# Wide products for the hi weights in the second feed-forward layer and the gated MLP, and a halved last block

## The chip, the cores and the metric

The kernel runs on one core of a Trainium2 chip. The metric is the device time in microseconds (us). TensorE (PE in the profile; PEld is its weight load) multiplies, VectorE (DVE) and ScalarE (ACT) work element by element, GpSimd (POOL) takes small powers and issues a few loads, SyncE (SP) issues the loads of the weights.

## What is computed

For 256 tokens of width 1024: a first block (feed-forward layer, a mixer of Fourier and differential attention branches, feed-forward layer, norm) and a second one (a gated MLP with token mixing, chunked attention, norm). The change touches two parts:

```python
def swiglu(x, wg, wu, wd):                       # 1024 -> 2816 -> 1024, used twice in the first block
    return (jax.nn.silu(x @ wg) * (x @ wu)) @ wd

def gmlp_mixer(h, w_in, ln_g, ln_b, w_s, b_s, w_out):
    u, v, z = jnp.split(h @ w_in, 3, axis=-1)    # 2048 each
    u = gelu(u); v = layer_norm(gelu(v), ln_g, ln_b)
    mixed = einsum('hts,bgshc->bgthc', masked w_s, v) + b_s
    return (u * mixed * silu(z)) @ w_out
```

## The kernel before

Every float32 operand is used as a sum of two parts of the faster type fp32r: hi (a copy in that type) and lo (what is left). A product of w and x is then three products: hi of w with hi of x, hi of w with lo of x, lo of w with hi of x. Weights pass in blocks of 1024 x 256 (or 256 x 1024), 1 MB each: SyncE loads a block into one of four `raw` buffers, ScalarE copies it into `hi` (`hi`, L290), VectorE subtracts it into `lo` (`lo`, L295); four slots of hi and lo each. A block's place in the order of all blocks is `NTH[...]`; the semaphores `hi`, `lo` and `used` count blocks. `hi` of block n waits until block n-4 has been multiplied.

The second feed-forward layer (`pe_ffn` with "ffn2") has 11 iterations. Iteration i multiplies gate block i into bank G and up block i into bank U (`to_features`, L330 to L332: for each half f of the block's 256 channels and each of 8 slices k of the width, three products of 256 columns, the tokens), then contracts down block i-1 with h of iteration i-1 into the four banks pAcc (`contract`, L380, 24 products of 512 columns). ScalarE takes silu of G into `stage_a`; VectorE multiplies U with it into h (L1526); ScalarE and VectorE split h into `h_hi` and `h_lo` (L930, L1329). Iteration 0 has the tokens as rows (`pair_to_tokens`), with gate and up block side by side in one product of 512 columns; its h is transposed through bank M in iteration 1. After the last iteration `contract_last` takes the first token tile of the last but one block (12 products), then the last block, whose h must be split by then; the turn to the next stage (residual sum, norm, transposes) is woven into it.

The gated MLP (`pe_gmlp`) first makes v (`vgate`, products of 512 columns in which xT is loaded and the weights of two blocks, two runs of 256, stream), then has 8 iterations: z block into G, transposition of W_s of this iteration into bank R (`w_s_transposed`, L691, plain float32), u block into U, mixing of tokens into bank M (`mix`, L701, plain float32, four products), contraction of block i-1. ScalarE: silu(z), a table load for gelu, gelu(u), a table load back. VectorE (`gated`): gelu(u) times silu(z) (L1770), b_s added to M (L1774), product of the two to h (L1778); then LayerNorm slices of the next v (`v_ln`), `lo` steps and the copies of W_s transposed (`w_s`). GpSimd loads the next W_s (L1925) once the last one is transposed, and the next LayerNorm slices (L1921) once b_s has been added; these stand in one queue in that order.

ScalarE, VectorE and GpSimd each follow an order written out by hand, and an instruction that waits holds all behind it.

Of the kernel before, what the change touches and what calls it, by code (L numbers as in the profile page):

```python
# [8 lines left out]
P = 128  # L9
TOK = 256  # L10
# [57 lines left out]
PAIR0 = {"mixin": 1, "ffn2": 2, "vgate": 3, "chunk": 7}  # L68
UNITS = [(0, 0), (0, 1), (1, 0), (1, 1), (2, 0), (2, 1), (4, 0), (4, 1), (3, 0), (3, 1),
# [15 lines left out]
def squares_done(g, t):  # L85
# [20 lines left out]
    "silu": "first gate (bank G) -> SA", "act_b": "second gate (bank U) -> SB", "h": "h in SBUF",  # L106
    "warm": "tables loaded ahead", "hh": "hi part of h", "hl": "lo part of h", "hT": "h of token-major blocks transposed",
# [20 lines left out]
    "a_mix": "tokens mixed", "a_zu": "b_s added", "a_ss": "gelu(u) * silu(z)",  # L128
# [8 lines left out]
def build(nc, T, out):  # L137
# [3 lines left out]
    with ctx:  # L141
# [21 lines left out]
        XT = [sb("xT_hi", KD * TOK, f32r), sb("xT_lo", KD * TOK, f32r)]  # L163
# [40 lines left out]
        BST = at("v_stats", NT * 4 * 6, f32, a0 + 14 * KB)  # L204

# [114 lines left out]
        def to_features(pe, n, bank, x, k0=0, nk=KD, half_way=0):  # L320

            wh, wl = v3(HI[n % NHL][:, :], KD), v3(LO[n % NHL][:, :], KD)
            for f in range(2):
                o = bank[:, f * TOK:(f + 1) * TOK]
# [133 lines left out]
        def pe_ffn(pe, ph, q, after=None):  # L458

            for i in range(NF):  # L460
# [14 lines left out]
                else:  # L475
                    if (ph, i) == ("ffn2", 1):
                        pe.wait_ge(S["pair_h"], 1)
                    else:
                        pe.wait_ge(S["silu"], H0[ph] + i)
                    to_features(pe, n, G, XT).then_inc(S["used"], 1)  # L480
                    pe.wait_ge(S["lo"], n + 2)
                    pe.wait_ge(S["h"], H0[ph] + i)
# [6 lines left out]
                    to_features(pe, n + 1, U, XT).then_inc(S["used"], 1)  # L489
# [172 lines left out]
        def pe_gmlp(pe):  # L662
# [31 lines left out]
            def mix(i):  # L694
# [4 lines left out]
                for h in range(2):  # L699
                    for g in range(NT):  # L700
                        end = pe.matmul(M[:, h * TOK + g * P:h * TOK + (g + 1) * P],  # L701
                                        VL[i % 2][:, g * BC + h * P:g * BC + (h + 1) * P], WT[:, h * P:(h + 1) * P],
                                        start=True, stop=True)
                end.then_inc(S["a_mix"], 1)

            for i in range(8):
# [4 lines left out]
                if i == 1:  # L711

                    mix(0)
# [4 lines left out]
                if i:  # L718
                    mix(i)
                if 0 < i < 7:  # L720
                    contract(pe, "gmlp", i - 1)
            contract_last(pe, "gmlp", 4)
# [242 lines left out]

        def act_ffn(act, ph):
            for i in range(NF):
# [31 lines left out]
            h_hi(act, ph, NF - 1)  # L999
# [187 lines left out]
        def act_gmlp(act):  # L1187
# [11 lines left out]
            for i in range(8):  # L1199
                n = NTH["gmlp", "z", i]  # L1200
                if i > 1:
                    hi(act, n + 3)
# [4 lines left out]
                if i != 1:  # L1207
# [3 lines left out]
                if i < 7:  # L1211
                    warm(act, ACT.Silu)
                    hi(act, n + 5)
                if i == 0:
                    hi(act, n + 6)
                h_hi(act, "gmlp", i)

# [283 lines left out]

        def dve_ffn(dve, ph):
            for i in range(NF):
# [229 lines left out]
        def dve_gmlp(dve):  # L1733
# [32 lines left out]

            def gated(i):
                dve.wait_ge(S["silu"], H0["gmlp"] + i + 1)
                dve.wait_ge(S["act_b"], ACT_B0["gmlp"] + i + 1)
                dve.tensor_tensor(SB[:, :], SB[:, :], SA[:, :], ALU.mult).then_inc(S["a_ss"], 1)  # L1770
                dve.wait_ge(S["a_mix"], i + 1)
                m4, x4 = (v[:, :].rearrange("p (h g t) -> p h g t", h=2, g=NT) for v in (M, MX))
                b_s = v3(APAR[i % 2][:, 2 * BC:3 * BC], 2).unsqueeze(2).broadcast_to([P, 2, NT, P])
                dve.tensor_tensor(x4, m4, b_s, ALU.add).then_inc(S["a_zu"], 1)  # L1774
                dve.wait_ge(S["a_ss"], i + 1)
                dve.wait_ge(S["a_zu"], i + 1)
                dve.wait_ge(S["hl"], H0["gmlp"] + i)
                dve.tensor_tensor(H[:, :], MX[:, :], SB[:, :], ALU.mult).then_inc(S["h"], 1)  # L1778

# [24 lines left out]
            lo(dve, n + 5)  # L1804
            gated(0)
# [3 lines left out]
            for i in range(1, 8):  # L1809
                n = NTH["gmlp", "z", i]  # L1810
                gated(i)
                if i < 7:
                    v_ln(i + 1)
                    lo(dve, n + 5)
                    h_lo(dve, "gmlp", i)
                    lo(dve, n + 6)
                    w_s(i + 1)
                    lo(dve, n + 7)
                else:
                    h_lo(dve, "gmlp", i)  # L1820
# [197 lines left out]
        def _(act):  # L2018
# [24 lines left out]
            act_ffn(act, "ffn2")  # L2043
            act_pair(act, NTH["vgate", "v", 0])
# [6 lines left out]
        def _(dve):  # L2051
# [16 lines left out]
            dve_ffn(dve, "ffn2")  # L2068
            dve_pair(dve, NTH["vgate", "v", 0])
# [39 lines left out]
```

## Time and profile before

| | us |
|---|---|
| Median of three runs | 883.17 (882.92 to 883.72) |
| Profiled execution | 882.84 |
| Its span, first to last instruction | 881.0 |
| TensorE busy in it | 867.2 (98%) |
| VectorE, ScalarE, GpSimd busy | 588.2, 479.5, 61.3 |

The profile is one execution. A line of a timeline gives start, length, engine, line of the kernel, operation, output and inputs; a product of TensorE runs into the next one, so what a product costs is the distance from one start to the next, not its length. "Idle before" is time in which the engine had nothing to do, with the instruction that ended it.

### The profile page before, as it was taken

The page shows a single profiled execution, that of the slowest core. Times are in us where ns is not written, and L with a number is a line of the kernel's source. Part 1 is how long each engine was busy: PE and PEld are TensorE (multiplying, and loading weights), DVE is VectorE, ACT ScalarE, POOL GpSimd, SP SyncE. Part 2 cuts the span into 40 slices and gives each one's busy share as a digit, 9 for nine tenths or more (in the row PEclk, how much of TensorE's full clock was granted, in tenths as well). Part 3 has the DMA queues.
Part 4 walks back from the last instruction along what each step waited for, and adds up shares of the span by engine and source line. Part 5 has one row for each costly group of instructions (what it writes and reads, how often), then busy time and mean ns, then how long its engine had stood idle before and what let it go on. Part 6 is the DMA issues. An engine that isn't in the chain of part 4 may idle for free. (4 is left out here: it accounts for less than half of the span.)

```text
span 881.0 us, 14413 instructions
## 1 busy us (share of the span) xinstructions
PE 867.2 (98%) x6150; PEld 809.1 (92%) x6150; DVE 588.2 (67%) x635; ACT 479.5 (54%) x591; POOL 61.3 (7%) x69
## 2 busy tenths in 40 slices
PE   7999999999999999999999999999999999999997
PEld 7999999998999999899999997989999997999995
DVE  5797988987587655655445457658766567666663
ACT  6667576656574443543443446447654645675652
POOL 0022223210000000000000000100000001000001
PEclk9999999999999999999999999999999999999999
DMA  9865556565644655556555655776656655854301
GB/s 299 303 201 188 191 191 192 181 204 156 201 145 138 197 192 167 174 185 195 187 191 181 202 165 170 224 248 221 218 188 213 219 149 174 264 167 156 121 1 48
DMA packets 124224, 163.14 MB, mean 185 GB/s; under 512 B 3969, under 2 KB 110977, under 8 KB 124161
## 3 DMA queue, kind: packets, MB, share of 16 engines
q1 hardware_dynamic: 122320, 155.41, 54.3%
q0 software_dynamic: 1552, 6.29, 2.1%
q8 instruction: 48, 0.79, 0.4%
q10 hardware_dynamic: 288, 0.52, 0.2%
q14 instruction: 16, 0.12, 0.0%
HBM read 161.17 MB, written 1.05 MB: 184 GB/s over the span
## 5 line engine op out<-in xcount | busy, mean ns | idle before, releaser
L295 DVE TENSOR_TENSOR lo<-raw,hi 128x2048 fp32r<-128x2048 f32 x131 | 299.1, 2288 | 136.2 <-ACT hi L290 136.1
L290 ACT ACTIVATE hi<-raw 128x2048 fp32r<-128x2048 f32 x140 | 265.3, 1905 | 28.7 <-DMA raw<-in_ffn_wd 7.2
L330 PE MATMUL pU<-xT_hi,hi 128*128 128x256 f32 x608 | 173.2, 285 | 0.0
L331 PE MATMUL pU<-xT_lo,hi 128*128 128x256 f32 x608 | 172.0, 283 | 0.0
L332 PE MATMUL pU<-xT_hi,lo 128*128 128x256 f32 x608 | 172.0, 283 | 0.0
L330 PE MATMUL pG<-xT_hi,hi 128*128 128x256 f32 x544 | 154.1, 283 | 0.0
L332 PE MATMUL pG<-xT_hi,lo 128*128 128x256 f32 x544 | 153.9, 283 | 0.0
L331 PE MATMUL pG<-xT_lo,hi 128*128 128x256 f32 x544 | 153.9, 283 | 0.0
L330 PEld LDWEIGHTS pU<-xT_hi,hi 128*128 128x128 f32 x608 | 116.6, 192 | 0.2
L331 PEld LDWEIGHTS pU<-xT_lo,hi 128*128 128x128 f32 x608 | 116.6, 192 | 0.0
L332 PEld LDWEIGHTS pU<-xT_hi,lo 128*128 128x128 f32 x608 | 116.6, 192 | 0.0
L330 PEld LDWEIGHTS pG<-xT_hi,hi 128*128 128x128 f32 x544 | 104.3, 192 | 1.5 <-issue 0.3
L331 PEld LDWEIGHTS pG<-xT_lo,hi 128*128 128x128 f32 x544 | 104.3, 192 | 1.1
L332 PEld LDWEIGHTS pG<-xT_hi,lo 128*128 128x128 f32 x544 | 104.3, 192 | 0.0
L930 ACT ACTIVATE h_hi<-h 128x512 fp32r<-128x512 f32 x28 | 17.7, 632 | 124.5 <-PE pAcc L380 119.1
L380 PE MATMUL pAcc<-hi,h_hi 128*128 128x512 f32 x240 | 74.9, 393 | 0.0
L380 PE MATMUL pAcc<-lo,h_hi 128*128 128x512 f32 x240 | 74.2, 390 | 0.0
L380 PE MATMUL pAcc<-hi,h_lo 128*128 128x512 f32 x240 | 74.0, 389 | 0.0
L380 PEld LDWEIGHTS pAcc<-hi,h_lo 128*128 128x128 f32 x240 | 45.1, 188 | 9.7
L380 PEld LDWEIGHTS pAcc<-lo,h_hi 128*128 128x128 f32 x240 | 45.0, 188 | 9.7
L888 POOL TENSOR_TENSOR stats<-stats,minus_half 128x1 f32<-128x1 f32 (+2 forms) x15 | 9.7, 647 | 580.7 <-DVE stats L882 275.6
L380 PEld LDWEIGHTS pAcc<-hi,h_hi 128*128 128x128 f32 x240 | 43.1, 189 | 7.1
(377 smaller groups left out, 1472.1 us busy)
## 6 DMA issues: line engine op xcount, KB each, us to landing
raw<-in_a_w_in SPq DMA_DIRECT2D x24, 1024.0 KB, 5.2
raw<-in_ffn_wd SPq DMA_DIRECT2D x22, 1024.0 KB, 5.0
raw<-in_ffn_wg SPq DMA_DIRECT2D x21, 1024.0 KB, 5.3
raw<-in_ffn_wu SPq DMA_DIRECT2D x21, 1024.0 KB, 5.3
raw<-in_w_in SPq DMA_DIRECT2D x16, 1024.0 KB, 5.4
raw<-in_a_w_out SPq DMA_DIRECT2D x8, 1024.0 KB, 5.0
raw<-in_w_kv SPq DMA_DIRECT2D x8, 1024.0 KB, 5.6
raw<-in_b_w_qz SPq DMA_DIRECT2D x8, 1024.0 KB, 5.7
```

Source lines behind the costliest of these rows:

```text
L290: act.activation(HI[n % NHL][:, :], RAW[n % NRAW][:, :], ACT.Copy).then_inc(S["hi"], 1)
L295: dve.tensor_tensor(LO[n % NHL][:, :], RAW[n % NRAW][:, :], HI[n % NHL][:, :].bitcast(f32), ALU.subtract).then_inc(S["lo"], 1)
L330: pe.matmul(o, wk, xh, start=(k == 0), stop=False)
L331: pe.matmul(o, wk, xl, start=False, stop=False)
L332: end = pe.matmul(o, wl[:, k0 + k, f * P:(f + 1) * P], xh, start=False, stop=(k == nk - 1))
L380: end = pe.matmul(ACC[2 * t + c][:, :], a, w[:, r, c * 512:(c + 1) * 512], start=(i == 0 and r == 0 and m == 0), stop=False, skip_group_ch ...
L888: pool.tensor_tensor(ST[:, c:c + w], ST[:, c:c + w], HALF[:, 0:w], ALU.pow).then_inc(S["rsqrt"], 1)
L930: act.activation(h_parts(ph, i)[0][:, :], H[:, :], ACT.Copy).then_inc(S["hh"], 1)
```

## The change

1. Wide products. In ffn2 from iteration 1 (gate) and 2 (up) on, and in the gated MLP from iteration 2 on (z, and u except the last), a block is multiplied by `wide_to_features`: hi of w meets hi and lo of x in one product of 512 columns (two runs of 256, 8 KB apart) into the whole of a bank, and lo of w meets hi of x in one of 256 columns onto the bank's left half. So each half f of a block has its own bank: gate (G, U), up (M, R), z (G, R), u (U, M). ScalarE copies the right half of each bank to SBUF (`wide_act`), VectorE adds the left half to it (`wide_dve`); silu, gelu and the products read the sum in `WG` or `WU`. 30 blocks are wide. Up block 1 goes to R by the old way.
2. Gated MLP, order. `mix(i)` writes bank G and stands with `w_s_transposed(i+1)` between u and the contraction; W_s of the next iteration is transposed there and no longer between z and u. VectorE adds b_s and multiplies with silu(z) first (`mixed`), and with gelu(u) afterwards (`gated`). The orders of `hi` and `lo` steps on ScalarE and VectorE change with it.
3. Last block of the gated MLP: `mix(7)` stands between z and u; u's halves go to banks U and R; gelu, h and its split are done a half at a time (`gated_last`).

```diff
-        XT = [sb("xT_hi", KD * TOK, f32r), sb("xT_lo", KD * TOK, f32r)]
+        XT_ALL = sb("xT", 2 * KD * TOK, f32r)
+        XT = [XT_ALL[:, c * KD * TOK:(c + 1) * KD * TOK] for c in range(2)]
...
+        def wide_to_features(pe, b, banks, free):
+            n = NTH[b]
+            wh, wl = v3(HI[n % NHL][:, :], KD), v3(LO[n % NHL][:, :], KD)
+            x4 = XT_ALL[:, :].rearrange("p (c k t) -> p c k t", c=2, k=KD)
+            for f, bank in enumerate(banks):
+                pe.wait_ge(*free[f])
+                for k in range(KD):
+                    w = slice(f * P, (f + 1) * P)
+                    pe.matmul(v3(bank[:, :], 2), wh[:, k, w], x4[:, :, k, :], start=(k == 0), stop=False,
+                              skip_group_check=True)
+                    end = pe.matmul(bank[:, 0:TOK], wl[:, k, w], x4[:, 0, k, :], start=False, stop=(k == KD - 1),
+                                    skip_group_check=True)
+                end.then_inc(S["used" if f else "wide"], 1)
...
+            mix(1, M)
+            w_s_transposed(2)
+            contract(pe, "gmlp", 0)
+            for i in range(2, 8):
+                z, u = ("gmlp", "z", i), ("gmlp", "u", i)
+                pe.wait_ge(S["lo"], NTH[z] + 1)
+                wide_to_features(pe, z, (G, R), ((S["silu"], H0["gmlp"] + 2) if i == 2 else (S["a_zu"], i),
+                                                 (S["a_wt"], 2 * (i + 1))))
+                pe.wait_ge(S["lo"], NTH[u] + 1)
+                if i < 7:
+                    wide_to_features(pe, u, (U, M), ((S["act_b"], ACT_B0["gmlp"] + 2), (S["a_zu"], 2)) if i == 2 else
+                                     [summed(("gmlp", "u", i - 1), f) for f in range(2)])
+                    pe.wait_ge(*summed(z, 0))
+                    mix(i, G)
+                    pe.wait_ge(*summed(z, 1))
+                    w_s_transposed(i + 1)
                     contract(pe, "gmlp", i - 1)
+                else:
+                    pe.wait_ge(*summed(("gmlp", "u", 6), 1))
+                    mix(7, M)
+                    pe.wait_ge(*summed(("gmlp", "u", 6), 0))
+                    pe.wait_ge(*summed(z, 1))
+                    to_features(pe, NTH[u], U, XT, other=R, first_half="wide").then_inc(S["used"], 1)
...
+        def wide_act(act, b, banks, dst, f):
+            if f:
+                act.wait_ge(S["used"], NTH[b] + 1)
+            else:
+                act.wait_ge(S["wide"], NTHW[b] + 1)
+            act.activation(dst[:, f * TOK:(f + 1) * TOK], banks[f][:, TOK:512], ACT.Copy).then_inc(S["wide_r"], 1)
+        def act_ffn2(act):
+            for i in range(1, NF):
+                gate, up = ("ffn2", "gate", i), ("ffn2", "up", i)
+                n = NTH[gate]
+                hi(act, n + LEAD)
+                act.wait_ge(S["h"], H0["ffn2"] + i)
+                wide_act(act, gate, (G, U), WG, 0)
+                wide_act(act, gate, (G, U), WG, 1)
+                if i == 1:
+                    h_hi(act, "ffn2", 0)
+                hi(act, n + 1 + LEAD)
+                act.wait_ge(*summed(gate, 1))
+                act.activation(SA[:, :], WG[:, :], ACT.Silu).then_inc(S["silu"], 1)
+                if i > 1:
+                    wide_act(act, up, (M, R), WU, 0)
+                    wide_act(act, up, (M, R), WU, 1)
+                if i < NF - 1:
+                    h_hi(act, "ffn2", i)
+                    hi(act, n + 2 + LEAD)
+            h_hi(act, "ffn2", NF - 1)
...
+        def wide_dve(dve, b, banks, dst, f):
+            dve.wait_ge(S["wide_r"], 2 * NTHW[b] + f + 1)
+            o = dst[:, f * TOK:(f + 1) * TOK]
+            dve.tensor_tensor(o, banks[f][:, 0:TOK], o, ALU.add).then_inc(S["wide_sum"], 1)
...
+            def gated_last():
+                dve.wait_ge(S["a_ms"], 8)
+                dve.wait_ge(S["last_u"], 1)
+                dve.wait_ge(S["hl"], H0["gmlp"] + 7)
+                dve.tensor_tensor(H[:, 0:TOK], MX[:, 0:TOK], SB[:, 0:TOK], ALU.mult).then_inc(S["last_h"], 1)
+                dve.wait_ge(S["last_hh"], 1)
+                dve.tensor_tensor(HL_LAST[:, 0:TOK], H[:, 0:TOK], HH_LAST[:, 0:TOK].bitcast(f32),
+                                  ALU.subtract).then_inc(S["last_hl"], 1)
...
+            for i in range(2, 8):
+                z, u = ("gmlp", "z", i), ("gmlp", "u", i)
+                n = NTH[z]
+                lo(dve, n + 3)
+                wide_dve(dve, z, (G, R), WG, 0)
+                wide_dve(dve, z, (G, R), WG, 1)
+                lo(dve, n + 4)
+                if i == 7:
+                    mixed(7, M)
+                    gated_last()
+                    break
+                wide_dve(dve, u, (U, M), WU, 0)
+                wide_dve(dve, u, (U, M), WU, 1)
+                mixed(i, G)
+                gated(i)
+                w_s(i + 1)
+                v_ln(i + 1)
+                lo(dve, n + 5)
+                h_lo(dve, "gmlp", i)
```

## Rows read from the trace of the kernel before

**Rows 1.** The page, busy time of the engines.
```profile
PE 867.2 (98%) x6150; PEld 809.1 (92%) x6150; DVE 588.2 (67%) x635; ACT 479.5 (54%) x591; POOL 61.3 (7%) x69
```
**Rows 2.** Waits of PE: who for whom, us in total, times, longest.
```profile
PE pAcc L380 <- DVE h_lo_last L1329: 1.1, 2, 0.8
PE pG L429 <- DVE xn L1698: 1.0, 1, 1.0
```
**Rows 3.** Timeline of PE, ffn2: up block starts, contraction starts, next gate starts.
```profile
509.65 0.28 PE L330 MATMUL pU<-xT_hi,hi 128*128 128x256 f32 x1
...
515.41 0.63 PE L380 MATMUL pAcc<-hi,h_hi 128*128 128x512 f32 x2
...
520.88 0.28 PE L330 MATMUL pG<-xT_hi,hi 128*128 128x256 f32 x1
```
**Rows 4.** Timeline of PE: 96 vgate products to z0; chunk's 24; chunk's K block.
```profile
569.58 0.40 PE L358 MATMUL pAcc<-hi,xT_hi 128*128 128x512 f32 x1
...
591.37 0.28 PE L330 MATMUL pG<-xT_hi,hi 128*128 128x256 f32 x1
...
744.56 0.40 PE L358 MATMUL pAcc<-hi,xTk_hi 128*128 128x512 f32 x1
...
750.16 1.04 PE L429 MATMUL pAcc<-ident,xn 128*128 128x128 f32 x8
...
752.02 0.28 PE L331 MATMUL pG<-xTk_lo,hi 128*128 128x256 f32 x1
...
757.58 0.28 PE L330 MATMUL pU<-xT_hi,hi 128*128 128x256 f32 x1
```
**Rows 5.** Timeline of PE, gated MLP's last iteration: u, mix, contractions of blocks 6 and 7.
```profile
718.44 0.36 PE L330 MATMUL pU<-xT_hi,hi 128*128 128x256 f32 x1
718.88 0.28 PE L330 MATMUL pU<-xT_hi,hi 128*128 128x256 f32 x1
...
724.27 1.05 PE L701 MATMUL pM<-wsT,v_ln 128*128 128x128 f32 x8
725.08 0.70 PE L380 MATMUL pAcc<-hi,h_hi 128*128 128x512 f32 x2
...
728.90 0.47 PE L380 MATMUL pAcc<-hi,h_hi_last 128*128 128x512 f32 x1 [0.82 <-DVE h_lo_last L1329]
```
**Rows 6.** Timelines of ACT and DVE in the same stretch.
```profile
724.47 0.60 ACT L1210 ACTIVATE stage_b<-pU 128x512 f32<-128x512 f32 x1 [2.05 <-PE pU L332]
...
728.06 0.69 DVE L1329 TENSOR_TENSOR h_lo_last<-h,h_hi_last 128x512 fp32r<-128x512 f32 x1 [0.70 <-ACT h_hi_last L930]
```
**Rows 7.** Timelines of ACT and DVE, ffn2's iteration 0: instructions on 256 columns of a bank.
```profile
367.82 0.39 ACT L978 ACTIVATE stage_a<-pU 128x256 f32<-128x256 f32 x1 [3.72 <-PE pU L360]
...
368.24 0.42 DVE L1522 TENSOR_TENSOR h<-pU,stage_a 128x256 f32<-128x256 f32 x1 [2.08 <-ACT stage_a L978]
```
**Rows 8.** Timelines of DVE, ACT and PE at the end of ffn2.
```profile
532.65 0.69 DVE L1526 TENSOR_TENSOR h<-pU,stage_a 128x512 f32<-128x512 f32 x1 [1.03 <-PE pU L332]
534.04 0.69 DVE L1329 TENSOR_TENSOR h_lo_last<-h,h_hi_last 128x512 fp32r<-128x512 f32 x1 [0.70 <-ACT h_hi_last L930]
...
533.37 0.63 ACT L930 ACTIVATE h_hi_last<-h 128x512 fp32r<-128x512 f32 x1 [4.08 <-DVE h L1526]
...
535.14 0.39 PE L380 MATMUL pAcc<-hi,h_hi_last 128*128 128x512 f32 x1
```
**Rows 9.** Load of W_s 2 in GpSimd's timeline, landing of all such loads, mix(1).
```profile
611.72 0.70 POOL L1925 DMA_DIRECT2D ws<-in_a_w_s  x1
...
DMA to landing us min/median/max: 4.4/5.4/8.0
...
615.71 1.05 PE L701 MATMUL pM<-wsT,v_ln 128*128 128x128 f32 x8
```
**Rows 10.** The page, costliest groups: busy us, mean ns | idle before, releaser.
```profile
L295 DVE TENSOR_TENSOR lo<-raw,hi 128x2048 fp32r<-128x2048 f32 x131 | 299.1, 2288 | 136.2 <-ACT hi L290 136.1
L290 ACT ACTIVATE hi<-raw 128x2048 fp32r<-128x2048 f32 x140 | 265.3, 1905 | 28.7 <-DMA raw<-in_ffn_wd 7.2
```

More of the change, by code:

```diff
@@ L68 @@
 PAIR0 = {"mixin": 1, "ffn2": 2, "vgate": 3, "chunk": 7}
+WIDE = [("ffn2", "gate", 1)] + [("ffn2", k, i) for i in range(2, NF) for k in ("gate", "up")]
+WIDE += [("gmlp", k, i) for i in range(2, 7) for k in ("z", "u")] + [("gmlp", "z", 7)]
+NTHW = {b: n for n, b in enumerate(WIDE)}
 UNITS = [(0, 0), (0, 1), (1, 0), (1, 1), (2, 0), (2, 1), (4, 0), (4, 1), (3, 0), (3, 1),
@@ L106 @@
     "silu": "first gate (bank G) -> SA", "act_b": "second gate (bank U) -> SB", "h": "h in SBUF",
+    "wide": "wide blocks half multiplied", "wide_r": "right halves of their banks -> SBUF",
+    "wide_sum": "left halves added to them (2 a block)",
+    "last_u": "second gate, first half of the last block of a phase", "last_h": "its h", "last_hh": "hi part", "last_hl": "lo part",
+    "a_ms": "mixed tokens times silu(z)",
     "warm": "tables loaded ahead", "hh": "hi part of h", "hl": "lo part of h", "hT": "h of token-major blocks transposed",
@@ L127 @@
     "a_wt": "and in SBUF (2 parts)", "a_vg": "(v - mean) * gain (2 tiles)", "a_vs": "v after LayerNorm (2 tiles)",
-    "a_mix": "tokens mixed", "a_zu": "b_s added", "a_ss": "gelu(u) * silu(z)",
+    "a_mix": "tokens mixed", "a_zu": "b_s added",
     "b_hb": "relative bias loaded", "b_mask": "chunk mask in it", "b_k": "K -> SBUF", "b_q": "Q -> SBUF",
@@ L488, in pe_ffn @@
                         end.then_inc(S["hT"], 1)
-                    to_features(pe, n + 1, U, XT).then_inc(S["used"], 1)
+                    if ph == "ffn1" or i == 1:
+                        to_features(pe, n + 1, U if ph == "ffn1" else R, XT).then_inc(S["used"], 1)
+                    else:
+                        free = [(S["h"], H0[ph] + 2)] * 2 if i == 2 else [summed((ph, "up", i - 1), f) for f in range(2)]
+                        wide_to_features(pe, (ph, "up", i), (M, R), free)
                 if 0 < i < NF - 1:
@@ L692, in w_s_transposed, with mix @@
                 end.then_inc(S["a_wt_ps"], 1)
-            def mix(i):
+            def mix(i, bank):
                 pe.wait_ge(S["a_vs"], 2 * (i + 1))
@@ L704, in mix @@
                 end.then_inc(S["a_mix"], 1)
-            for i in range(8):
+            for i in range(2):
                 n = NTH["gmlp", "z", i]
@@ L711, in pe_gmlp @@
                 if i == 1:
-                    mix(0)
+                    mix(0, M)
                 w_s_transposed(i)
@@ L1198, in act_gmlp @@
                 hi(act, n + 5)
-            for i in range(8):
+            for i in range(2):
                 n = NTH["gmlp", "z", i]
-                if i > 1:
-                    hi(act, n + 3)
                 act.wait_ge(S["used"], n + 1)
@@ L1808, in dve_gmlp @@
             lo(dve, n + 6)
-            for i in range(1, 8):
-                n = NTH["gmlp", "z", i]
-                gated(i)
[L1812 to L1820, printed above, removed]
+            n = NTH["gmlp", "z", 1]
+            mixed(1, M)
+            gated(1)
+            w_s(2)
+            v_ln(2)
+            lo(dve, n + 5)
+            h_lo(dve, "gmlp", 1)
+            for i in range(2, 8):
+                z, u = ("gmlp", "z", i), ("gmlp", "u", i)
+                n = NTH[z]
+                lo(dve, n + 3)
[9 more added lines that the diff above has]
+                mixed(i, G)
+                gated(i)
+                w_s(i + 1)
+                v_ln(i + 1)
+                lo(dve, n + 5)
+                h_lo(dve, "gmlp", i)
         def b_softmax(dve, i):
```

116 lines of the change are left out of this document (90 added, 26 removed).

## The prediction

> **What bounds the kernel now.** I read the page first: TensorE is busy for 867.2 of 881.0 us, the others for two thirds of it at most [rows 1]. A busy TensorE need not be at its peak, so next the waits: it waits for others for about a microsecond at a time, at the turns between stages [rows 2], and never inside the iterations. The kernel is a chain of TensorE's products, and the time changes by what the products cost from start to start and by waits that come or go at a few places. The start-to-start cost is read from timelines. In ffn2 an up block of 48 narrow products (256 columns) runs from 509.65 to 515.41: 5.76 us, 120 ns each; a contraction of 24 products of 512 columns runs from there to 520.88: 5.47 us, 228 ns each [rows 3]. A product of twice the columns is thus 12 to 13 ns cheaper than two narrow ones: each carries a fixed part of about 13 ns, whatever its length.
>
> **Wide products.** A step (one k, one f) is 3 x 120 = 360 ns now. The narrow product that stays costs 120 ns. The wide one streams two runs of 256 columns of xT. Nothing now streams xT in 512 columns; the nearest rows are vgate's, with the operands in the opposite roles but with two runs: 96 products from 569.58 to 591.37, 227 ns each [rows 4]. So 227 + 120 = 347 ns, 13 ns less. Steps: ffn2 19 blocks, gated MLP 11, 16 steps a block, 480 in all: 480 x 13 ns = 6.24 us less. Bounds: at the start of the chunk stage the same form costs 233 ns (24 products, 744.56 to 750.16), and the narrow products that follow 118 (47 of them, 752.02 to 757.58) [rows 4], so 6 to 15 ns a step, 2.9 to 7.2 us; at the worst, two narrow ones' 240, nothing. I take vgate's value, since xT and the slots of hi and lo lie where they lie now; chunk's row has another buffer (xTk). The change from a wide to a narrow product is taken at no extra cost: the contraction's 228 and the block's 120 include such borders [rows 3].
>
> **The new copies and sums.** A wide block adds two ScalarE copies of 256 columns, 0.39 us each, and two VectorE sums, 0.42 us [rows 7]: 1.6 us an iteration on each engine in ffn2. They are off TensorE's path if they are done before the bank is needed. In ffn2 (time from the iteration's start): h_hi, which waits for the contraction, then a hi step of 1.9 us (down block), another 1.9 (the next gate block), so ScalarE is free at about 4.4; gate's second half ends at 5.6, is copied by 6.1, and VectorE, which by then has its lo steps of 2.3 us [rows 10] done at 7.0, has summed at 7.8. TensorE needs G and U again at 16.6. The hi and lo steps queued behind these waits (up i+1, down i) end at 8.0 and 10.3, and at 2.4 and 4.7 of the next iteration; they are needed when TensorE reaches those blocks, at 22 and 28. 6 us or more of cover everywhere, so nothing. SyncE's loads wait for lo steps, which come no later than now. In the gated MLP the nearest need is z's sums, behind which mix(i) now stands in TensorE's queue: ready at 6.6, wanted at 11.1. If this 4.5 us were gone, each us more would be TensorE's.
>
> **One switch less.** The first fp32r product after a float32 one holds the engine longer: u's first three take 0.44 us (718.44 to 718.88) where three take 0.36 elsewhere [rows 5], so 0.08. W_s is now transposed next to mix, six times: 6 x 0.08 = 0.48 us less (between 0 and 0.6).
>
> **The last block of the gated MLP.** Now from u's end (724.27) to the contraction of block 7 (728.90) pass 4.63 us: mix 0.81, a switch 0.08, 12 products of 0.228 = 2.73, and 1.01 of wait and restart [rows 5]. With mix ahead of u and halves, after u come gelu (starts 0.20 after u's end [rows 6]), h, hi, lo, each on 256 columns, about 0.4 with 0.04 between them, and 0.15 until TensorE starts (728.06 + 0.69 to 728.90 [rows 5, 6]): 2.1 us, under 2.73. So the 1.01 goes. But TensorE must wait before u for the sum of z's second half: 0.20 + 0.39 + 0.04 + 0.42 + 0.15 = 1.20 after z's end, of which mix covers 0.81: 0.39 us more. Net 0.62 less.
>
> **The turn of ffn2.** Its last h isn't halved, and a copy (0.39), a sum (0.42) and handoffs (0.07 to 0.09) now stand before it: 0.88 us. h_lo ends at 534.73, TensorE takes up the last block at 535.14 [rows 8]; after the 0.15 there are 0.26 us of cover. The rest, 0.62, is a wait of TensorE. But the chain of the turn on ScalarE and VectorE (hi, lo, residual sums, norm) starts from h_hi and is late by 0.88, and TensorE waits for its end already now (1.0 us for xn [rows 2]). So all 0.88 us count.
>
> **W_s of block 2.** It was transposed inside iteration 2; now TensorE wants it right behind mix(1), at 615.71 + 0.81 = 616.52. GpSimd issues its load at 611.72, after the LayerNorm slices that wait for b_s being added; 5.4 us to landing: 617.1 [rows 9]. VectorE adds b_s a little earlier (the product that stood before it moves behind), at most 0.7. Behind the wait stands the contraction of block 0. Landing between 4.4 and 8.0 us [rows 9] gives 0 to 3.2 us; I take 0.7. Later W_s have an iteration of cover.
>
> **Sum.** -6.24 - 0.48 - 0.62 + 0.88 + 0.7 = -5.76 us. The profiled execution took 882.84 us around a span of 881.0, and the median is 883.17, 0.33 more. So a profile of 877.1 and a median of 877.4.
>
> **Rivals.** (A) The sum as it stands: 877.4. Chance 0.73.
> (B) The wide product costs what chunk's does, 233 to 234 ns: a step saves 6 ns, 480 x 6 = 2.9 us instead of 6.24: 880.8. For it: the same form has both prices in one trace, so the price hangs on where the operands lie, and xT has never streamed this way. Against: xT's narrow products cost as much streamed as loaded, 120. Chance 0.13.
> (C) The fixed 13 ns isn't saved: it belongs to 256 columns that stream (a run, or the weight load beside it), and the wide product costs 240. Then only the other terms are left: -0.48 - 0.62 + 0.88 + 0.7 = +0.5, so 883.7, no change. Against: vgate's and the contraction's rows both have 227 to 228. Chance 0.09.
> The Trainium skill, in "TensorE: Matmul & The Clock Gate", section "Back-to-back issue gap", gives a warm product its columns at 2.4 GHz plus a fixed 2.5 ns. By that a step saves 2.5 ns, an estimate of 1.2 us for 480 steps, and the time would be 882.5. The trace disagrees at 256 and 512 columns alike (120 and 227 ns against the page's 109 and 216); only the size of the part that goes with a product differs.
> (D) Slower: late sums. In the gated MLP z's sums stand behind a hi and a lo step, and mix, W_s and the contraction behind the sums. If weight blocks land late, each us beyond the 4.5 of cover falls on TensorE. ScalarE waited 7.2 us for a load once in this trace [rows 10]; at that lateness in each of the five iterations 2 to 6 it is 2.7 x 5 = 13.5 us: 890.9. It decides from 6.0 us of lateness an iteration (1.5 x 5 = 7.5 beyond the cover makes it slower by 0.2%). Against: the 28.7 us that ScalarE waits at hi steps are spread over 140. Chance 0.05.
>
> **Range and chances.** About 0.2% (1.8 us) is what a measurement of this kernel can tell from no change. Within (A), the narrow product at 118 and no wait for W_s take off 1.7, a W_s load at its slowest adds 2.5. The range reaches to (B): 875.2 to 881.0. Faster: (A), (B): 0.86. Same: (C): 0.09. Slower: (D): 0.05.
>
> **What the profile would show.** A block of z or gate takes 5.55 us instead of 5.76 from its first start to the next block's; in (B) 5.66, in (C) 5.76. No wait of TensorE inside the iterations; an iteration of ffn2 16.6 us instead of 17.0. Waits of TensorE: about 0.6 for h_lo_last in ffn2 and none in the gated MLP; 1.2 for xn; one for the sum of z 7 (0.4); one behind mix(1) (0.7), before a W_s transposition. The prediction is wrong if the wide products have a price of their own, or if TensorE waits at each mix.

## The result, and the profile after

| | before | after |
|---|---|---|
| median (lowest to highest), 7 runs each | 883.48 us (882.91 to 883.72) | 880.00 us (879.87 to 880.64) |
| profiled execution: time, span | 882.84, 881.0 us | 880.00, 878.2 us |

The ratio is 0.9963, with a 95% interval of 0.9954 to 0.9973: 0.4% faster, by 3.5 us between the medians (2.4 to 4.1 by the interval). The forecast was 877.4, the range 875.2 to 881.0. The time lies in the range, but near rival (B)'s 880.8 and not at the point.

The page of after, the engines' busy time (before: [rows 1]), and its waits of PE (before: [rows 2]):

```profile
PE 865.6 (99%) x5670; PEld 784.5 (89%) x5670; DVE 610.5 (70%) x697; ACT 500.1 (57%) x653; POOL 61.2 (7%) x69
```

```profile
PE pG L463 <- DVE xn L1844: 1.2, 1, 1.2
PE pAcc L414 <- DVE h_lo_last L1443: 0.7, 2, 0.4
```

480 products fewer, and TensorE busy for 1.6 us less: the products that went gave back little. The timeline of PE in ffn2 (columns as in [rows 3]); gate block's first bank, four products in the middle of it, up block's first bank, contraction, next gate block:

```profile
401.85 0.39 PE L359 MATMUL pG<-xT,hi 128*128 128x512 f32 x1
...
402.54 0.40 PE L359 MATMUL pG<-xT,hi 128*128 128x512 f32 x1
402.78 0.28 PE L361 MATMUL pG<-xT,lo 128*128 128x256 f32 x1
402.90 0.40 PE L359 MATMUL pG<-xT,hi 128*128 128x512 f32 x1
403.14 0.28 PE L361 MATMUL pG<-xT,lo 128*128 128x256 f32 x1
...
407.49 0.40 PE L359 MATMUL pM<-xT,hi 128*128 128x512 f32 x1
...
413.14 0.64 PE L414 MATMUL pAcc<-hi,h_hi 128*128 128x512 f32 x2
...
418.65 0.39 PE L359 MATMUL pG<-xT,hi 128*128 128x512 f32 x1
```

A wide block takes 5.64 us (401.85 to 407.49) and 5.65 (to 413.14), where 5.55 was forecast, 5.66 for rival (B), and 5.76 was the narrow one's [rows 3]; an iteration takes 16.80 us (401.85 to 418.65), where 16.6 was forecast. A step is 11.29 / 32 = 353 ns: in the rows a wide product is followed after 240 ns and a narrow one after 120. The exact starts in the trace repeat over three steps, 236 + 113, 233 + 117, 241 + 120 ns. So a wide product between narrow ones costs 233 to 241 ns, and the narrow one 117 on average, where vgate's row had promised 227 and the block's row 120.

Where the 2.8 us of the two spans went is read from landmarks. Of before, rows that don't stand above: start of gate 1, of the last contraction pair of ffn2, of the norm's transpositions, of z 2, and the end of z 7 (the W_s transposition behind it):

```profile
367.62 0.28 PE L330 MATMUL pG<-xT_hi,hi 128*128 128x256 f32 x1
...
532.39 0.63 PE L380 MATMUL pAcc<-hi,h_hi 128*128 128x512 f32 x2
...
543.11 0.66 PE L429 MATMUL pG<-ident,xn 128*128 128x128 f32 x4 [1.00 <-DVE xn L1698]
...
622.09 0.28 PE L330 MATMUL pG<-xT_hi,hi 128*128 128x256 f32 x1
...
718.31 0.38 PE L691 MATMUL pR<-ident,ws 128*128 128x128 f32 x2
```

The same landmarks of after, with the start of the last block's contraction in ffn2 and, at the end of the gated MLP, mix(7), u 7, and the contractions of blocks 6 and 7:

```profile
367.77 0.39 PE L359 MATMUL pG<-xT,hi 128*128 128x512 f32 x1
...
530.70 0.40 PE L414 MATMUL pAcc<-hi,h_hi 128*128 128x512 f32 x1
...
534.00 0.47 PE L414 MATMUL pAcc<-hi,h_hi_last 128*128 128x512 f32 x1 [0.36 <-DVE h_lo_last L1443]
...
542.23 0.44 PE L463 MATMUL pG<-ident,xn 128*128 128x128 f32 x2 [1.18 <-DVE xn L1844]
...
621.42 0.39 PE L359 MATMUL pG<-xT,hi 128*128 128x512 f32 x1
...
716.50 1.05 PE L742 MATMUL pM<-wsT,v_ln 128*128 128x128 f32 x8
717.68 0.36 PE L342 MATMUL pU<-xT,hi 128*128 128x256 f32 x1
...
723.50 0.63 PE L414 MATMUL pAcc<-hi,h_hi 128*128 128x512 f32 x2
...
726.25 0.39 PE L414 MATMUL pAcc<-hi,h_hi_last 128*128 128x512 f32 x1
```

| stretch | before | after | difference |
|---|---|---|---|
| start of the kernel to gate 1 | 367.62 | 367.77 | +0.15 |
| ffn2's iterations (19 wide blocks), to the last contractions | 164.77 | 162.93 | -1.84 |
| turn, to the norm's transpositions | 10.72 | 11.53 | +0.81 |
| to z 2 (holds W_s 2's transposition in after) | 78.98 | 79.19 | +0.21 |
| gated MLP, z 2 to z 7's end (11 wide blocks) | 96.22 | 95.08 | -1.14 |
| to the contraction of block 7 (holds W_s 7's in before) | 10.59 | 9.75 | -0.84 |
| to the end | 152.1 | 151.95 | -0.15 |

The sum is -2.80. The two stretches with wide blocks give 2.98, where 6.24 (and 0.48 for the merge) were forecast.

### The profile page after: what moved, and what is told of

Its sections match the earlier page's. It is cut to its first block, busy times and chain, and to the rows that moved or that the text cites. A ratio compares the mean times of both kernels' runs of the same rounds, so it can differ in the third digit from the quotient of the medians.

```text
span 878.2 us, 13599 instructions
## 1 busy us (share of the span) xinstructions
PE 865.6 (99%) x5670; PEld 784.5 (89%) x5670; DVE 610.5 (70%) x697; ACT 500.1 (57%) x653; POOL 61.2 (7%) x69
## 4 chain that ended last, share of the span: by engine, by line
PE 94%; DVE 3%; DMA 1%; ACT 1%; issue 1%; SPq 0%; POOL 0%; POOLq 0%; DVEq 0%
PE pAcc L414 22%; PE pU L342 5%; PE pU L343 5%; PE pU L344 5%; PE pG L342 5%; PE pG L344 5%; PE pG L343 5%; PE pG L359 3%; PE pU L359 3%; PE pR L359 3%; PE pM L359 3%; PE pG L361 2%; PE pAcc L392 2%; PE pAcc L393 2%; PE pAcc L394 2%; PE pU L361 2%
## 5 line engine op out<-in xcount | busy, mean ns | idle before, releaser
L342 PE MATMUL pU<-xT,hi 128*128 128x256 f32 x360 | 102.5, 285 | 0.1
L343 PE MATMUL pU<-xT,hi 128*128 128x256 f32 x360 | 101.8, 283 | 0.0
L344 PE MATMUL pU<-xT,lo 128*128 128x256 f32 x360 | 101.8, 283 | 0.0
L342 PE MATMUL pG<-xT,hi 128*128 128x256 f32 x288 | 81.7, 284 | 0.0
L344 PE MATMUL pG<-xT,lo 128*128 128x256 f32 x288 | 81.5, 283 | 0.0
L343 PE MATMUL pG<-xT,hi 128*128 128x256 f32 x288 | 81.5, 283 | 0.0
L342 PEld LDWEIGHTS pU<-xT,hi 128*128 128x128 f32 x360 | 69.0, 192 | 0.5 <-DVE wide_gate L1620 0.3
L343 PEld LDWEIGHTS pU<-xT,hi 128*128 128x128 f32 x360 | 69.1, 192 | 0.0
L344 PEld LDWEIGHTS pU<-xT,lo 128*128 128x128 f32 x360 | 69.0, 192 | 0.0
L342 PEld LDWEIGHTS pG<-xT,hi 128*128 128x128 f32 x288 | 55.2, 192 | 0.8 <-issue 0.3
L343 PEld LDWEIGHTS pG<-xT,hi 128*128 128x128 f32 x288 | 55.2, 192 | 0.5
L344 PEld LDWEIGHTS pG<-xT,lo 128*128 128x128 f32 x288 | 55.2, 192 | 0.0
L1443 DVE TENSOR_TENSOR h_lo<-h,h_hi 128x512 fp32r<-128x512 f32 x28 | 19.3, 688 | 48.9 <-ACT h_hi L990 48.9
```

Of the source, the lines that this page charges most:

```text
L1443: dve.tensor_tensor(b[:, :], src[:, :], a[:, :].bitcast(f32), ALU.subtract).then_inc(S["hl"], 1)
```

## The experiments

"The kernel before" was run beside each group: its median was 883.51 us beside e1 to e4, 883.62 beside e5 to e8, 883.15 beside e9 to e11 and 883.08 beside e12. Every ratio is to the kernel before of the same group. "Theory" with a number or letter means the one of that name in the expectation just above. The diffs are shortened.

**e1_grouped.** Is it the alternation of wide and narrow products?

```diff
                 for k in range(KD):
                     w = slice(f * P, (f + 1) * P)
                     pe.matmul(v3(bank[:, :], 2), wh[:, k, w], x4[:, :, k, :], ...)
+                for k in range(KD):
                     end = pe.matmul(bank[:, 0:TOK], wl[:, k, w], x4[:, 0, k, :], ...)
```

> The changed kernel, but in each half of a wide block the eight wide products come first and the eight narrow ones after them. In the changed kernel a step of one wide and one narrow product costs 353 ns (236 and 117), where 347 (227 and 120) were forecast. Theory 1: the price comes from the alternation of the two lengths. Then eight wide ones in a row cost 227 each and the narrow ones 120, a block 5.55 us instead of 5.65, and the time is 880.0 - 30 x 0.10 = 877. Theory 2: it comes from what the wide product streams (two runs of xT, 8 KB apart). Then a wide one costs 234 or more in a row as well, a block stays at 5.65 and the time at 880.0.

Measured: 877.47 us (877.45 to 877.99), ratio to before 0.9935 (0.9919 to 0.9952), 2.5 us under the changed kernel. The timeline of PE, same iteration:

```profile
401.51 1.98 PE L359 MATMUL pG<-xT,hi 128*128 128x512 f32 x8
403.33 1.11 PE L362 MATMUL pG<-xT,lo 128*128 128x256 f32 x8
404.28 2.00 PE L359 MATMUL pU<-xT,hi 128*128 128x512 f32 x8
406.12 1.12 PE L362 MATMUL pU<-xT,lo 128*128 128x256 f32 x8
...
412.66 0.63 PE L415 MATMUL pAcc<-hi,h_hi 128*128 128x512 f32 x2
```

Behind the 512-column contraction eight wide products take 1.82 us, 227 ns each, just as vgate's did; eight narrow ones 0.95; behind these, eight wide ones 1.84. Two blocks are 11.15 us. So the wide product of this xT has vgate's price in a run, and it is the alternation with shorter products that costs.

**e2_one_run.** Is it the two runs of 256 columns? The wide product streams 512 adjacent columns instead: hi, or lo, of two neighbouring slices k. The sizes stay, but the sums are no longer the product that the kernel should make.

```diff
-                    pe.matmul(v3(bank[:, :], 2), wh[:, k, w], x4[:, :, k, :], ...)
+                    pe.matmul(bank[:, :], wh[:, k, w], XT_ALL[:, k * 512:(k + 1) * 512], ...)
```

> The changed kernel, but the wide product streams 512 columns that lie in one run (hi or lo of two neighbouring slices k) instead of hi and lo of one slice: the same sizes on wrong data, so what the blocks compute is not the product. Theory 1 (alternation): a step stays at 353 ns. Theory 2 (two runs): 347 ns, a block 5.55 us, the time 877.

Measured: 879.97 us (a single run), a span of 878.2, the changed kernel's to the tenth, and the starts repeat as there (233 + 118, 241 + 120, 236 + 113 ns). The form of the operand has no price here.

**e3_split.** The change without its wide products: each is two narrow ones again, all else is as changed.

```diff
-                    pe.matmul(v3(bank[:, :], 2), wh[:, k, w], x4[:, :, k, :], ...)
+                    pe.matmul(bank[:, 0:TOK], wh[:, k, w], x4[:, 0, k, :], ...)
+                    pe.matmul(bank[:, TOK:512], wh[:, k, w], x4[:, 1, k, :], start=False, ...)
```

> The changed kernel with all its orders, banks, copies and sums, but each wide product is made as two narrow ones. If only the products carry the gain, a wide block is back at 5.76 us (3 x 120 a step) and the time is 880.0 + 30 x 0.105 = 883.2, the same as the kernel before: the rest (turn of ffn2 +0.8, last block of the gated MLP -0.7) cancels out. Rival: the orders and the halved block gained something that the products do not show; then the time is under 882.5.

Measured: 884.49 us (884.04 to 885.3), ratio 1.0014 (1.0004 to 1.0023), 0.98 us over before and 1.3 over the 883.2 expected, which had left out the wait for W_s 2 (0.9, below). The prediction's terms without the products and the merge give +0.88 - 0.62 + 0.7 = +0.96. That the medians meet this sum is in part chance, since the term for W_s is 0.9 here and not 0.7: GpSimd's timeline, then PE's.

```profile
612.66 0.71 POOL L2107 DMA_DIRECT2D ws<-in_a_w_s  x1
```

```profile
616.87 1.05 PE L744 MATMUL pM<-wsT,v_ln 128*128 128x128 f32 x8
618.64 0.44 PE L734 MATMUL pR<-ident,ws 128*128 128x128 f32 x2 [0.72 <-DMA ws<-in_a_w_s]
```

Mix to W_s is 1.77 us, 0.9 more than mix alone takes in after (0.88, below); from its issue to its use the load had 6.0 us. The stretch from the norm's transpositions to z 2 is 80.13 us, 0.94 more than in after. Of the 4.5 us between this kernel and the changed one, this is 0.9; the two stretches with wide blocks (164.77 and 96.29 us) are 3.05 longer, and that is what the wide products bring, 6.4 ns a step.

**e4_last_up_narrow.** The turn of ffn2: the last up block goes the old way, into bank R, with no copy and no sum ahead of h (this line picks the wide blocks; the products, ScalarE's copies and VectorE's h follow it).

```diff
-WIDE = [("ffn2", "gate", 1)] + [("ffn2", k, i) for i in range(2, NF) for k in ("gate", "up")]
+WIDE = [("ffn2", "gate", 1)] + [("ffn2", k, i) for i in range(2, NF) for k in ("gate", "up") if (k, i) != ("up", NF - 1)]
```

> The changed kernel, but the last up block of ffn2 is multiplied the old way, into one bank (R), and VectorE takes h from that bank without copy and sum. If the 0.8 us that the turn of ffn2 lost come from copy and sum in front of the last h, the last contraction starts 2.75 us after the up block as in the kernel before and the transpositions 0.81 us earlier; the block costs 0.1 more: 879.3. If the turn is held by something else, 880.1.

Measured: 879.65 us (879.54 to 880.06), ratio 0.9959 (0.9944 to 0.9974). Timeline of PE:

```profile
530.71 0.63 PE L414 MATMUL pAcc<-hi,h_hi 128*128 128x512 f32 x2
...
533.46 0.39 PE L414 MATMUL pAcc<-hi,h_hi_last 128*128 128x512 f32 x1
...
541.42 0.66 PE L463 MATMUL pG<-ident,xn 128*128 128x128 f32 x4 [1.00 <-DVE xn L1846]
```

The turn is 10.71 us again, as in before (10.72) and not as in after (11.53), and the wait for h_lo_last is gone. So the copy and the sum are what delayed the turn. The median shows 0.35 of these 0.8 us, too little to tell from after by the ratios alone; the landmarks account for it. The narrow block costs 0.1 more, and the stretch to z 2 is 0.4 longer (79.58 us against 79.19), since in this execution TensorE waited for W_s 2 (0.2 us in its list of waits).

**e5_whole_block, e6_block_and_last, e7_fours.** How the price of alternation is made up. e5 has all 16 wide products of a block first, then the 16 narrow ones; e6 is e5 with the narrow last up block of e4.

```diff
             for f, bank in enumerate(banks):
                 pe.wait_ge(*free[f])
                 for k in range(KD):
                     pe.matmul(v3(bank[:, :], 2), wh[:, k, f * P:(f + 1) * P], x4[:, :, k, :], ...)
+            for f, bank in enumerate(banks):
+                for k in range(KD):
                     end = pe.matmul(bank[:, 0:TOK], wl[:, k, f * P:(f + 1) * P], x4[:, 0, k, :], ...)
```

> In every wide block the 16 wide products (both halves, both banks) come first and the 16 narrow ones after them; nothing else differs from the changed kernel. Theory 1, the price lies at each return from narrow to wide products: in the trace of the kernel with halves grouped, the first five wide products after eight narrow ones took 233, 236, 228, 233 and 230 ns and the first narrow one 113, so one return costs 25 - 7 = 18 ns. A block has one return instead of two, 30 blocks x 18 ns = 0.5 us less than the grouped kernel's 877.5: 876.9. Theory 2, the price lies in how long the second bank's narrow half is kept open or in late sums (a first half is ready 1.9 us later): no gain or a loss, 877.5 or more, with waits of TensorE inside the iterations.

> The kernel of e5_whole_block, and the last up block of ffn2 multiplied in the old narrow way into bank R, so that nothing stands between its second gate and h. If the two gains are independent: the turn gives back what it gave in the kernel with the last up block narrow (879.65 against 880.0, 0.35), so 0.35 less than e5_whole_block, 876.5; TensorE waits 0.3 for h_lo_last once (gates stage) instead of twice. If the turn is set by another chain after grouping, it equals e5_whole_block.

e7 has the groups of e1 cut in two (k 0 to 3 wide, then narrow, then k 4 to 7):

```diff
-                for k in range(KD):
+                for k0 in (0, KD // 2):
+                    for k in range(k0, k0 + KD // 2):
```

> Groups of four: in each half 4 wide, 4 narrow, 4 wide, 4 narrow products; four returns to wide a block instead of two (grouped) or sixteen (changed kernel). Theory 1a, each return costs 18 ns as read from the grouped kernel's trace: 30 blocks x 2 x 18 ns = 1.1 us over 877.5: 878.6, a block of 5.60 us. Theory 1b, the price is the same for each return, 880.0 - 877.5 = 2.5 us over 30 x 14 returns = 6 ns: 877.9, a block of 5.57 us.

| | returns from narrow to wide for each block | median, us (lowest to highest) | ratio to before |
|---|---|---|---|
| e5 | 1 | 876.84 (876.76 to 877.55) | 0.9926 (0.9914 to 0.9939) |
| e6 | 1 | 876.82 (876.58 to 877.19) | 0.9925 (0.9912 to 0.9937) |
| e1 | 2 | 877.47 (877.45 to 877.99) | 0.9935 (0.9919 to 0.9952) |
| e7 | 4 | 878.59 (878.21 to 878.95) | 0.9944 (0.9931 to 0.9958) |
| changed kernel | 16 | 880.00 (879.87 to 880.64) | 0.9963 (0.9954 to 0.9973) |

(A gate or z block follows a contraction, also of 512 columns, and has one return less than the table says.) e5 and e7 came out as theory 1 and 1a had it (876.9 and 878.6): each return costs about 18 ns as long as the runs are four or more long (20 from e1 to e5 and 15 from e1 to e7, by the two stretches with wide blocks), and where every product is a return it is 6 ns a step, 96 a block. The rows of e5, an up block, and of e7, a half gate block:

```profile
406.82 2.00 PE L358 MATMUL pM<-xT,hi 128*128 128x512 f32 x8
408.66 1.98 PE L358 MATMUL pR<-xT,hi 128*128 128x512 f32 x8
410.47 1.12 PE L362 MATMUL pM<-xT,lo 128*128 128x256 f32 x8
```

```profile
401.45 1.07 PE L360 MATMUL pG<-xT,hi 128*128 128x512 f32 x4
402.36 0.64 PE L363 MATMUL pG<-xT,lo 128*128 128x256 f32 x4
402.83 1.09 PE L360 MATMUL pG<-xT,hi 128*128 128x512 f32 x4
403.76 0.63 PE L363 MATMUL pG<-xT,lo 128*128 128x256 f32 x4
```

In e5, 1.84 us for the eight behind narrow ones, 1.81 for the eight behind wide ones; in e7 0.91 for four behind the contraction, 0.93 for four behind narrow ones. e6 should have been at 876.5; at 0.02 under e5 its last narrow block shows no gain that can be told. Its turn is 0.82 us shorter than e5's (10.71 against 11.53), but ffn2's iterations are 0.19 longer with the narrow block (161.09 against 160.90), and the stretch to z 2, in which it waited for W_s 2 and e5 did not, 0.40 (79.64 against 79.24). What is left, 0.23, is less than the runs of one kernel scatter.

**e8_before_moved.** The prediction had seen the same product at 227 and at 233 and put it on the operands' place. Both kernels allocate xT on a multiple of 128 bytes (worked out from the order and sizes of the regions); xTk begins 96 bytes past one. Here the kernel before has xT moved by 32 bytes.

```diff
+        region(32)
         XT = [sb("xT_hi", KD * TOK, f32r), sb("xT_lo", KD * TOK, f32r)]
+        region(32)
```

> The kernel before, with 32 bytes left free ahead of xT_hi and 32 behind xT_lo, so that xT begins 32 bytes past a multiple of 64 as xTk does; every other buffer behind them stays on its place modulo 64. Theory P, the place of the streamed buffer sets the price (xTk: 118 and 233 ns; xT: 120 and 227 ns): a narrow block of 48 goes from 5.76 to 5.68 us, some 75 blocks, 6 us less, the 168 products of vgate and mixin that stream xT's partner or use it as weights change at most 1 us: 877 to 879. Theory Q, the place plays no part: 883.5, narrow products still 120 ns.

Measured: 875.77 us (875.62 to 876.14), ratio 0.9912 (0.9897 to 0.9927): 7.9 us from 64 bytes of padding, more than twice what the change brings. It is theory P, and 1.2 us under the least that P gave: the narrow product falls to 117 ns and not 118.

```profile
410.16 0.62 PE L382 MATMUL pAcc<-hi,h_hi 128*128 128x512 f32 x2
...
415.75 0.28 PE L332 MATMUL pG<-xT_hi,hi 128*128 128x256 f32 x1
```

The narrow block (404.56 to 410.16) takes 5.60 us, 117 ns a product; but the contraction takes 5.59 instead of 5.47 [rows 3]. h_hi and h_lo had moved by 64 bytes with everything behind xT.

**e9_before_xt_only, e10_after_xt_only, e11_best_xt_only.** xT alone is moved, in the kernel before, in the changed kernel, and in e6.

```diff
-        XT = [sb("xT_hi", KD * TOK, f32r), sb("xT_lo", KD * TOK, f32r)]
...
+        HALF = sb("minus_half", 4)
+        XT = [sb("xT_hi", KD * TOK, f32r), sb("xT_lo", KD * TOK, f32r)]
         IDENT = sb("ident", P)
         ST = sb("stats", 112)
-        HALF = sb("minus_half", 4)
```

> The kernel before, with xT alone on another place: it is allocated behind h_lo and the 32 bytes of minus_half, so it begins 32 bytes past a multiple of 128, and hi, lo, h_hi, h_lo and everything from xTk on keep their places modulo 2048. In e8_before_moved everything behind xT had also moved by 64 bytes, and the products of the contractions took 231 and 236 ns in turn instead of 227. Theory H, that price came with the moved h_hi and h_lo: narrow products of xT at 117, contractions at 227 again, 720 products x 5 ns = 3.6 us less than e8's 875.8: 872.2. Theory X, xT's place alone sets the state of all: contractions stay at 233, 875.8.

> The changed kernel with the same move of xT. Theory 1, the gain of the wide product hangs on xT's place: where a narrow product takes 117, two of them take 234, what a product of 512 columns takes there (231 to 236), so the wide products save nothing and what is left of the change is what e3_split showed (+1.2 us against before at most, W_s load and start in it): e9_before_xt_only plus 0 to 1.2 us. Theory 2, the fixed part of a product is saved wherever xT lies: 3 to 6 us under e9_before_xt_only.

> The fastest order so far (wide products of a block first, narrow ones after, last up block of ffn2 narrow) with the same move of xT. Theory 1: grouping saves nothing either, as no wide product is cheaper than two narrow ones there: within 0.5 us of e10_after_xt_only. Theory 2: 3 us under e10_after_xt_only, as 876.8 is under 880.0 on the old place.

| | median, us (lowest to highest) | ratio to before |
|---|---|---|
| e9, narrow | 872.40 (872.37 to 872.65) | 0.9877 (0.9863 to 0.9892) |
| e10, wide, alternating | 871.58 (871.11 to 871.93) | 0.9869 (0.9852 to 0.9885) |
| e11, wide, grouped | 873.20 (872.70 to 873.73) | 0.9886 (0.9871 to 0.9901) |

Timelines of PE in ffn2: e9 (up block, contraction, next gate), e10 (a half block, contraction), e11 (16 wide, then 8 narrow).

```profile
402.35 0.28 PE L330 MATMUL pU<-xT_hi,hi 128*128 128x256 f32 x1
...
407.94 0.63 PE L380 MATMUL pAcc<-hi,h_hi 128*128 128x512 f32 x2
...
413.41 0.28 PE L330 MATMUL pG<-xT_hi,hi 128*128 128x256 f32 x1
```

```profile
404.81 0.39 PE L359 MATMUL pR<-xT,hi 128*128 128x512 f32 x1
...
407.58 0.39 PE L414 MATMUL pAcc<-hi,h_hi 128*128 128x512 f32 x1
```

```profile
397.36 2.03 PE L358 MATMUL pG<-xT,hi 128*128 128x512 f32 x8
399.23 2.03 PE L358 MATMUL pU<-xT,hi 128*128 128x512 f32 x8
401.09 1.10 PE L362 MATMUL pG<-xT,lo 128*128 128x256 f32 x8
402.04 1.10 PE L362 MATMUL pU<-xT,lo 128*128 128x256 f32 x8
```

The stretches with wide blocks, measured as in the table of the result:

| us | ffn2's iterations | gated MLP, z 2 to z 7's end |
|---|---|---|
| e9 | 161.65 | 94.57 |
| e10 | 160.72 | 94.03 |
| e11 (last up block narrow) | 161.85 | 94.59 |

e9: the block is 5.59 us and the contraction 5.47 again: theory H. e10: eight steps in 2.77 us, 346 ns, where three narrow ones are 349 to 350. By the stretches wide products save 1.47 us here, 3 ns a step, and the rest of the change takes 0.2 (after) to 1.0 (e3) of them back. Measured are 0.8 between the medians, though the ratios' intervals overlap. e11: a run of eight wide ones takes 1.87 us, 234 ns each, so a step is 234 + 118 = 352 and the stretches are as long as the narrow kernel's. In this place the alternation is the cheaper of the two orders: its stretches are 1.7 us shorter than e11's. (The medians differ by 1.6, but two other things stand between them: TensorE waited 1.0 us for W_s 2 in e11 and not in e10, and e11's turn is 0.8 shorter.) In the old place it was the other way round.

Theory 2 falls for both. Theory 1 is not met either: e10 is 0.8 us under e9, where 0 to 1.2 over it was expected, and e11 is 1.6 from e10, where 0.5 at most was. What stands of it is its premise for runs: there two narrow products (2 x 117) cost what a wide one does (234). It had not reckoned that alternating the wide one costs less, 228 to 230 ns from start to start in e10.

**e12_before_xt_64.** Which multiple matters?

```diff
-        XT = [sb("xT_hi", KD * TOK, f32r), sb("xT_lo", KD * TOK, f32r)]
...
-        IDENT = sb("ident", P)
         ST = sb("stats", 112)
+        XT = [sb("xT_hi", KD * TOK, f32r), sb("xT_lo", KD * TOK, f32r)]
+        IDENT = sb("ident", P)
```

> The kernel before with xT alone moved again, now behind the 448 bytes of stats: it begins 64 bytes past a multiple of 128 (in e9_before_xt_only 32 bytes past one, 117 ns; in the kernel before on one, 120 ns). Theory 64: all multiples of 64 are alike, narrow products of xT stay at 120 and vgate's at 227: 883.2. Theory 128: only multiples of 128 have these prices, since h_hi and h_lo, moved by 64 bytes in e8_before_moved, had made the contractions dearer: narrow products at 117, vgate's at 233, as in e9_before_xt_only: 872.4.

Measured: 871.53 us (871.44 to 872.75), ratio 0.9871 (0.9854 to 0.9887). It is theory 128, 0.9 us under its time: 64 bytes past a multiple of 128 is as good as 32. The first vgate product and z 0:

```profile
562.13 0.40 PE L358 MATMUL pAcc<-hi,xT_hi 128*128 128x512 f32 x1
...
584.12 0.28 PE L330 MATMUL pG<-xT_hi,hi 128*128 128x256 f32 x1
```

96 products in 21.99 us, 229 ns each: not the 233 expected, but between it and 227. That a buffer must begin on a multiple of 128 to have the price of 120 and 227 is not shown: only one such place of xT was tried.

## Why the prediction was right, and where it was wrong

The direction and the range held, and the terms for the last block and for the turn; the largest term came out at half its size, the merge of W_s with mix at nothing. That the time still lies in the range is in part luck: its upper end was set by rival (B), whose reason isn't the one that acted, and a wait of 0.7 us that was counted did not come. The sign that the prediction had named against itself, that the wide products have a price of their own, was seen.

**Wide products: the mechanism stood, the term was mis-sized.** Forecast -6.24, measured -2.98 in the two stretches. The step that failed is the price of the product. The prediction took vgate's 227 ns for the wide product, "since xT and the slots of hi and lo lie where they lie now". That is so in a run (e1), but no row of before shows a 512-column product between 256-column ones, and the prediction took the change of length "at no extra cost: the contraction's 228 and the block's 120 include such borders". They include one border in 24 or 96 products; 18 ns a return is under 1 ns a product there, and 6 ns a step where every second product is one. It could have been read before: behind the narrow up block the contraction of [rows 3] starts its first products after 233, 236, 229, 232 and 231 ns, the same as e1's wide ones behind narrow ones (234, 235, 229, 232, 231), and only then after 227. The time is near rival (B)'s; its reason, the place of the operands, is a real one (e8 to e12) but not the cause here, since at this place the wide product does cost 227. Rival (C) is refuted by e1 (227 ns in a run) and by e3, where two narrow products for each wide one make the two stretches 3.05 us longer.

**The fixed part of a product.** The Trainium skill, in "TensorE: Matmul & The Clock Gate", section "Back-to-back issue gap", was quoted for a fixed part of 2.5 ns a product; that section gives it for a product by itself and says that a stream of weight loads and products, as here, goes otherwise. The runs show no one figure: twice the narrow product's price less the wide one's is 13 ns where xT lies on a multiple of 128 bytes and wide products stand in runs (2 x 120 - 227), 7 ns alternating there (360 - 353), 3 alternating in the other place (e10), and nothing in runs there (2 x 117 - 234, e11).

**Copies and sums: right.** TensorE waits nowhere inside the iterations. Gate's second sum in ffn2 (timeline of DVE) ends 7.8 us after the iteration's start at 401.85, as forecast:

```profile
409.27 0.41 DVE L1620 TENSOR_TENSOR wide_gate<-pU,wide_gate 128x256 f32<-128x256 f32 x1
```

Rival (D) didn't occur; nothing was late.

**The merge of W_s with mix: wrong.** Forecast -0.48, measured nothing. The rows behind mix(1) in after, with the contraction:

```profile
614.83 1.05 PE L742 MATMUL pM<-wsT,v_ln 128*128 128x128 f32 x8
615.71 0.38 PE L732 MATMUL pR<-ident,ws 128*128 128x128 f32 x2
615.85 0.70 PE L414 MATMUL pAcc<-hi,h_hi 128*128 128x512 f32 x2
```

From mix to what follows are 0.88 us, where 0.81 stood before [rows 5]. The exact starts show why. In before the last product of mix is followed after 31 ns by the contraction, in after 112 ns by the transposition; all that stand before it take 108 to 112. The transpositions are as long in both (109 and 28 ns), and so is the contraction's first product (313 and 314). So a run of float32 products has a short last one before fp32r products, and a first fp32r product behind it that is longer (201 ns instead of 120 at u). The prediction counted the second, 0.08 us less, and not the first: one run of float32 products instead of two also has one short end less, 0.08 more. e3 confirms the sum: with narrow products its stretch from z 2 to z 7's end is 96.29 us against 96.22.

**The last block of the gated MLP: right.** Mix(7) and its wait take 1.18 us (716.50 to 717.68); 0.39 of wait beyond 0.81 had been forecast, 1.20 in all. From u's end to the contraction of block 7 pass 2.75 us, no wait, as forecast. The stretch gives 0.84; 0.21 of it is W_s 7's transposition, which had moved ahead of z 2 in kind (the +0.21 there). Net 0.63, forecast 0.62.

**The turn of ffn2: right.** +0.81 against +0.88. The last block's contraction starts 3.30 us behind the last pair instead of 2.75, of which 0.36 is in the list as the wait for h_lo_last (0.62 had been forecast for it); the wait for xn is 1.18, and 1.2 was forecast. With e4 the cause is shown.

**W_s of block 2: right in mechanism, absent in the profile of after.** GpSimd issued the load at 610.61, and it landed 4.9 us later, 0.2 before TensorE wanted it at 615.71. That differs from execution to execution: the same load took 5.4 us in e4 (a wait of 0.2), 5.9 in e3 (0.7) and 6.1 in e11 (1.0). The prediction took 0.7 out of 0 to 3.2.

**The sum with the measured terms:** -2.98 for the products, 0 for the merge, -0.63 for the last block, +0.81 for the turn, 0 for W_s, and 0.0 at the two ends of the kernel (+0.15, -0.15) give -2.80. The forecast was -5.76, 2.96 more: 3.26 for the products and 0.48 for the merge, less 0.7 for a wait that didn't come and 0.08 at the turn and the last block. The time is off by 2.6 and not 2.96, since the profiled execution of after took what its median is, and not 0.33 less.

## What to carry to other kernels

Price a product from a row in which it has the neighbours that it will have; a run's price is not the price of alternation, and grouping products of one length is worth a try where banks and slots allow it. But the order and the place in SBUF have to be tried together: here the best order in one place (e6) is the slower of the two wide ones tried in the other (e11 against e10), and starting one buffer 64 bytes past a multiple of 128, without the change, took 11.6 us off (e12, 871.5), over three times the change's gain. Before removing a switch between two types, look at the starts on both sides of it: what follows may be dearer and what precedes it cheaper.

## What the runs showed of the hardware

With fp32r operands, a weight load for each product and a granted clock of 0.996 to 1.00 over the span (the upper level, 2.4 GHz), from start to start:

| xT begins | 256 columns in a run | 512 in a run | a wide-narrow step, alternating |
|---|---|---|---|
| on a multiple of 128 bytes | 120 (before) | 227 (vgate, e1) | 353 (after) |
| 32 past it | 117 (e9) | 233 (e9's vgate), 234 (e11) | 346 (e10) |
| 64 past it | 117 to 118 (e12) | 229 (e12's vgate) | not tried |
| 96 past it (xTk) | 118 [rows 4] | 233 [rows 4] | not tried |

"64 past it" and the others name the start modulo 128 bytes. xTk, moved from 96 to 32 past in e8, went from 118 to 117 ns as well.

The buffer sets the price as streamed operand (narrow blocks) and as loaded one (vgate). h, which is loaded too, does the same: contractions take 227 to 228 ns a product with h_hi on a multiple of 128 and 233 in e8, with h_hi 64 bytes past it. But xT 64 bytes past it is at 229 as the loaded one (e12), so the start modulo 128 doesn't settle the price alone; what else does is not shown. That a price falls for 256 columns and rises for 512 at the same move was not expected, and its cause is open: the records show starts and durations, not what the engine waits for inside.
